# Interleaving the last Strassen products of a hybrid conv/retention layer by token block, and moving its norm steps and weight copies

## What is computed

```python
hcat = x @ w_in                                   # (S, 3584): B, C, h | q, k, v, g
y_conv = b_gate * causal_short_conv(c_gate * hc, conv_w)
o = chunkwise_retention(rotary(q), rotary(k) * 128 ** -0.5, v)     # 4 heads of 128
y_ret = silu(g) * head_group_norm(o, ...)
mix = concatenate([y_conv, y_ret]) @ w_out
x = layer_norm(ALPHA * x + mix, ln1_w, ln1_b)
ff = square(relu(x @ w_ff1)) @ w_ff2              # 1024 -> 4096 -> 1024
ple = sigmoid(x @ w_ple_gate) * (p @ w_ple_proj)  # 256 -> 1024
x = layer_norm(ALPHA * x + ff + ple, ln2_w, ln2_b)
```

## Time and profile before

| what | value |
|---|---|
| device time, median of 3 runs | 792.77 us (791.97 to 793.96) |
| time of the profiled execution | 793.19 us |
| its span, first to last instruction, slowest core | 791.5 us |
| PE busy on that core | 754.2 us (95%) |
| DVE busy | 545.9 us (69%) |
| ACT busy, POOL busy | 304.3 us (38%), 186.7 us (24%) |
| mean rate of the DMA engines | 163 GB/s |

### The profile page before, as it was taken

How to read it: one execution, slowest core, us unless ns; L and a number is a source line. 1 busy time by engine, 2 the same in 40 slices (tenths; PEclk the granted TensorE clock), 3 DMA queues, 4 the chain that set the end, 5 groups by cost and what they waited for, 6 DMA issues and landing times.

```text
span 791.4 us, 12329 instructions; the slowest of 8 cores (787.0 to 791.5 us)
## 1 busy us (share of the span) xinstructions
PE 757.0 (96%) x3896; PEld 357.0 (45%) x3896; DVE 546.3 (69%) x762; ACT 304.3 (38%) x620; POOL 186.3 (24%) x223
## 2 busy tenths in 40 slices
PE   3999999999989999999999999999999999899994
PEld 1444445555545445444444444454444444344441
DVE  4565955648875697798349878835788877765667
ACT  2222226564656307656552100022766752100431
POOL 9100025764455401111110000000443440000011
PEclk9999999999999999999999999999999999999998
DMA  9998048999996251567979668476498676176412
GB/s 130 161 172 186 28 133 107 134 107 113 116 121 202 100 176 55 198 265 251 247 205 157 156 199 200 171 212 188 112 252 274 212 256 224 54 166 146 141 80 107
DMA packets 30352, 128.94 MB, mean 163 GB/s; under 512 B 3728, under 2 KB 5904, under 8 KB 23568
## 3 DMA queue, kind: packets, MB, share of 16 engines
q0 software_dynamic: 9840, 50.34, 39.3%
q1 hardware_dynamic: 19584, 76.23, 28.5%
q10 hardware_dynamic: 864, 1.57, 0.7%
HBM read 131.27 MB, written 45.09 MB: 223 GB/s over the span
## 4 chain that ended last, share of the span: by engine, by line
PE 87%; DVE 5%; DMA 2%; issue 2%; POOL 2%; ACT 1%; DVEq 0%; ACTq 0%; POOLq 0%
PE ps L194 85%; DMA xT_56<-xT 2%; PE ps L198 2%; DVE xacc L212 1%; DVE ycat L201 1%; DVE xacc L201 0%; POOL wc_59 L236 0%; DVE ring_111 L201 0%; POOL wc_60 L236 0%; POOL xT_55 L236 0%; POOL xT_56 L236 0%; ACT sqj L223 0%; POOL lnst L201 0%; DVE tR_143 L201 0%; DVE ra_78 L201 0%
## 5 line engine op out<-in xcount | busy, mean ns | idle before, releaser
L201 DVE TENSOR_TENSOR xacc<-xacc,ps 128x512 f32<-128x512 f32 x80 | 53.0, 685 | 55.7 <-PE ps L194 54.4
L201 POOL TENSOR_TENSOR lnst<-lnst,neghalf 128x1 f32<-128x1 f32 x32 | 26.9, 840 | 138.9 <-DVE lnst L205 87.8
L194 PE MATMUL ps<-ring_106,ycat 128*128 128x512 bf16 x256 | 59.5, 379 | 0.0
L194 PE MATMUL ps<-ring_104,ycat 128*128 128x512 bf16 x224 | 53.1, 388 | 2.6 <-DVE tR_143 L201 2.6
L223 ACT ACTIVATE ycat<-ps 128x1024 bf16<-128x1024 bf16 x16 | 16.3, 1020 | 90.6 <-PE ps L198 90.6
L194 PE MATMUL ps<-ycat,ring_108 128*128 128x512 bf16 x208 | 48.0, 379 | 0.0
L194 PE MATMUL ps<-ycat,ring_109 128*128 128x512 bf16 x208 | 47.8, 379 | 0.0
L201 DVE TENSOR_TENSOR ycat<-hT 128x2048 bf16<-128x2048 bf16 x36 | 43.4, 1222 | 1.5
L201 POOL TENSOR_TENSOR hT<-tR_140 128x512 bf16<-128x512 f32 x15 | 17.5, 1167 | 113.1 <-ACT tR_140 L223 113.1
L194 PE MATMUL ps<-ycat,ring_106 128*128 128x512 bf16 x176 | 41.1, 379 | 0.0
L223 ACT ACTIVATE sg_138<-xacc 128x512 f32<-128x512 f32 x14 | 8.8, 628 | 78.3 <-DVE xacc L201 68.9
(11 more groups left out here) (352 smaller groups left out, 1601.6 us busy)
## 6 DMA issues: line engine op xcount, KB each, us to landing
s_wb<-w_ff POOLq DMA_DIRECT2D x8, 1024.0 KB, 30.4
out<-xacc SPq DMA_DIRECT2D x14, 512.0 KB, 3.4
s_w<-ring_104 SPq DMA_DIRECT2D x10, 512.0 KB, 3.5
s_w<-ring_105 SPq DMA_DIRECT2D x10, 512.0 KB, 3.8
xtmp<-x SPq DMA_DIRECT2D x8, 512.0 KB, 7.3
ring_106<-s_wb POOLq DMA_DIRECT2D x4, 1024.0 KB, 7.7
s_x1f<-xtmp SPq DMA_DIRECT2D x8, 512.0 KB, 4.4
xacc<-s_x1f SPq DMA_DIRECT2D x8, 512.0 KB, 6.2
```

The costliest lines, as they stand in the source:

```text
L194: self.P.op("pe", lambda e: e.matmul(out, lhsT=lhsT, rhs=rhs, start=start, stop=stop, skip_group_check=skip), reads, writes)
L201: self.P.op(eng, lambda e: e.tensor_tensor(out=out, in0=in0, in1=in1, op=op), reads, writes)
```

## The change

- **Copies.** Three of the ten weight copies are issued in the convolution, behind units (2,3), (3,1) and (3,3), the other seven at the end of the retention iterations t = 0, 1, 2, 4, 5, 12 and 13. Each names the tile behind whose write it stands.
- **Norm steps.** In `phase_ff1_last` the stages n = 4, 8 and 12 emit two pieces of the background queue instead of one, and one more piece is emitted behind `last_sums(15)`. All 18 pieces of `gen_outs` then stand ahead of the gate.
- **Last phase.** M1, M3 and M6 stay. M2 and M4 alternate group by group; then come M5_0, M5_1, M7_0, M5_2, M7_1, M7_2, M5_3 (product and token group). The last group, M7_3, runs as two halves of 256 columns in banks 7 and 6, each subtracted and put into the statistics by itself; the statistics of block 3 are four BN_STATS of 256 columns on DVE. `gen_last` waits one piece less before its first operation. M7's slabs are loaded into the ring slots that M2's slabs leave.

The core of the diff:

```diff
-        def copy_bf16(k):
-            h.dma("pool", s_wb[k], w_ff1[k] if k < 8 else w_gate[k - 8], ("wc", k // 4, k % 4), [],
-                  [("s_wb", k)])
+        copies = [0, 4, 1, 5, 2, 6, 3, 7, 8, 9]
+        def copy_bf16(after):
+            k = copies.pop(0)
+            h.dma("pool", s_wb[k], w_ff1[k] if k < 8 else w_gate[k - 8], ("wc", k // 4, k % 4),
+                  [after], [("s_wb", k)])
...
             conv((tt, j))
+            if (tt, j) in ((2, 3), (3, 1), (3, 3)):
+                copy_bf16(("ycat", tt * 4))
...
-            if 1 <= t <= 10:
-                copy_bf16((0, 4, 1, 5, 2, 6, 3, 7, 8, 9)[t - 1])
+            if t in (0, 1, 2, 4, 5, 12, 13):
+                copy_bf16(("kr", t % 2))
...
                 if n >= 2:
-                    bg.step()
+                    bg.step(1 + (n % 4 == 0))
...
             last_sums(15)
+            bg.step()
             product(15, "M6", p, True)
...
-            for m in PRODS[s_]:
+            order = [(m, p, j) for m in ("M1", "M3", "M6") for j, p in JP]
+            groups = [(m, p) for p in range(4) for m in ("M2", "M4")]
+            groups += [("M5", 0), ("M5", 1), ("M7", 0), ("M5", 2), ("M7", 1), ("M7", 2), ("M5", 3)]
+            order += [(m, p, j) for m, p in groups for j in range(2)]
+            slabs = {}
+            for m, p, j in order:
...
+                if (m, j) not in slabs:
+                    slabs[m, j] = use_slab(m, j, min(slab_n["use"] + 5 + (m != "M1"), 30))
+                ff2_product(s_, m, j, p, *slabs[m, j])
+                if j == 1:
+                    ff2_adds(s_, m, p)
+                    if m == "M2":
+                        act_stats(4 + p, 1)
+                        prefetch(30 + 2 * (p == 3))
+                    if m == "M4":
+                        act_stats(4 + p, 0)
+                        bg.add(gen_last(4 + p))
+                    if m == "M5" and p < 3:
+                        act_stats(p, 1)
+                    if m == "M7":
+                        act_stats(p, 0)
+                        bg.add(gen_last(p))
+                bg.step(2 + ((m, p, j) == ("M5", 3, 0)))
+            ff2_add(3, 0, BANK[1]["M5"] + 3, -1)
+            last_stats(3, 2)
+            last_stats(3, 3)
+            for q in range(2):
+                qs = slice(q * 256, (q + 1) * 256)
+                for c in range(16):
+                    lt, rl = left(s_, "M7", c, 3)
+                    slab, rs = slabs["M7", c // 8]
+                    h.mm(ps[7 - q][:, 0:256], lt, slab[:, c % 8, qs], c == 0, c == 15, rl + rs,
+                         [RP[7 - q]])
+                v = xacc[:, 3, qs]
+                h.tt("dve", v, v, ps[7 - q][:, 0:256], ALU.subtract, [RP[7 - q], ("xa", 3)],
+                     [("xa", 3)])
+                last_stats(3, q)
+                if q == 0:
+                    bg.step()
+            bg.add(gen_last(3))
...
             if b != 3:
-                for _ in range(3):
+                for _ in range(2):
                     yield
```

More of the change, by code:

```diff
@@ L1349, in phase_ff2_last @@
                     bg.add(sums[ahead[m]])
-                if m in sums:
+                    del ahead[m]
+                if sums.get(m) in bg.gens:
                     bg.until(sums[m])
[L1352 to L1370, removed]
+                if (m, j) not in slabs:
+                    slabs[m, j] = use_slab(m, j, min(slab_n["use"] + 5 + (m != "M1"), 30))
@@ L1374, in load_x2b, with last_stats @@
                   ("x2b", b % 2), [("s_x1", b)], [("x2b", x2i(b))])
[L1376 to L1380, removed]
+        st24 = lnst[:, 6:8, :].rearrange("p a b -> p (a b)")[:, 0:24]
+        def last_stats(b, k):
+            P.op("dve", lambda e: e.bn_stats(out=st24[:, k * 6:(k + 1) * 6],
+                                             in_=xacc[:, b, k * 256:(k + 1) * 256]),
+                 [("xa", b)], [("lnst", 6), ("lnst", 7)])
         def act_stats(b, hf):
@@ L1402, in gen_last @@
             else:
-                yield from last_stats(b, 0)
-                P.op("dve", lambda e: e.bn_aggr(out=mv, in_=lnst[:, b, 0:12]), [rl], [("mv", b)])
+                P.op("dve", lambda e: e.bn_aggr(out=mv, in_=st24), [("lnst", 6), ("lnst", 7)],
+                     [("mv", b)])
                 h.ts("dve", rstd, mv[:, 1:2], LN_EPS, ALU.add, [("mv", b)], [("rstd", b)])
```

## The result

The changed kernel takes 829.87 us (median of 4 runs, 828.16 to 832.0) against 792.84 us before: a ratio of 1.0468, 95% interval 1.0437 to 1.0498. I had forecast 791.2 us with 787.6 to 796.6; it is 37 us slower. In some executions the cores of one die show a lower granted clock and the time is some per cent longer; every median here leaves these out.

The account below looks back on a forecast made before the run. PE was taken as the bound. Core 0's 791.5 - 1.6 - 2.9 - 1.0 + 1.0 + 0.6 + 2.0 gave 789.6, core 6 789.9; plus 1.7 for the execution, less 0.4 for the median: 791.2 us, range 787.6 to 796.6.

Parts of the forecast that it names:

- The copies: Weight copies issued earlier, in two groups: POOL issues them in idle time, only a load beside them could be late; 0, bounds -1.7 to +1.7.
- The double steps: Two norm pieces at n = 4, 8, 12 delay bank sums: PE waits 1.0 at n = 4, 0.6 for both others.
- the two waits at the end of `phase_ff1_last`: PE's waits for bank sums on DVE go, with no norm piece in stage 15: -1.0 us, bounds 0 and -1.0.
- SP's queue: In `phase_ff1_last`, ring pieces stand behind load1 and out2/load2, which wait for stores to land: +2.0 us, bounds 0 to 7.
- The gate's end: PE's wait ahead of M1 shrinks to 1.20 and the clock stays up: -2.9 us on core 0, -0.5 on core 6.
- The tail: Behind PE's last matmul, the new last-phase order lets DVE end earlier: -1.6 us, bounded by DVE, not PE.
- a thing that would make me wrong: Sign against the forecast: PE waits in the new last phase for banks that DVE has not emptied; no size given.
- The sum: Whole kernel: core 0 ends at 789.6 and core 6 at 789.9, giving a median of 791.2 us.
- The rival of the full stall: On SP, a store's landing holds the pieces fully, at out1 and again at n = 12: 797.6 us, slower; chance 0.20.
- a clock that falls in a new wait: Rival: one core's clock falls again in a new PE wait, costing 1.5 us: 792.7; forecast with fallen clock has chance 0.42.

## Why the prediction was wrong

**The copies.** The step that failed is "The copies", which said that POOL's issue time lies in its idle time and that "a load beside them" was all that could be late: 0, bounds -1.7 and +1.7. I took `[after]` as a mark for the place in POOL's queue. It is a read, and the kernel's bookkeeping lets the next write of that tile wait for its readers, a transfer's until it has landed. The number for that was there, 29.9 us to land, and the loop writes `kr` again after two iterations. I did not set the one beside the other. The read costs 30.3 us with the rest of the change around it (829.9 to 799.6), 28 alone; with the same places and no read it costs nothing. On core 6 the sum is 6.5 + 0.8 + 9.5 = 16.8 of the waits for `kr` (the fourth, 1.1, has its like before), 6.8 at the convolution's end and 8.1 for the clock: 31.7.

**The double steps** were in the sum at 1.6 us and measured 5.7 on core 0 with the copies put back: 1.96, 1.95 and 1.82 behind n = 4, 8 and 12. At n = 4 the 1.0 was the stall without POOL's power; the 0.9 for it stood in the bound and should have been in the sum. 0.57 of what was missing is that wait, and some 0.6 is the second operation, which took 1.92 us and not the 1.28 of the one row I had read; among the eight blocks of core 0 before it took 1.28 to 2.16 (what this hangs on is not shown). At n = 8 and 12 I took 0.6 for both, on the ground of "more slack", from no row; they cost nearly as much as the first. And of the two waits at the end of `phase_ff1_last`, in the sum at -1.0, one of 0.51 is left, so that term came out as -0.5.

**SP's queue.** The mechanism was right and so were both places: load1 waits for out1 (13.1 us) and load2 for out2, and the pieces that M6(8) and M7(8) need stand behind. The size was too small, and it differs by core. With the copies put back there is no such wait on five cores, and there are 3.3, 4.7 and 6.3 us on the other three, where I had 2.0 for all and 0 to 7 as bounds. PE on the slowest, core 4:

```profile
603.15 4.48 PE L194 MATMUL ps<-ycat,ring 128*128 128x512 bf16 x20 [2.98 <-DMA ring<-s_w]
613.51 5.30 PE L194 MATMUL ps<-ycat,ring 128*128 128x512 bf16 x15 [3.28 <-DMA ring<-s_w]
```

On these three cores one bank wait of 1.95 is gone, so that much only changes its name. Behind the second wait 15 matmuls take 5.30 us where they take 3.61 on other cores, at a granted clock of 0.68 in 613.5 to 618.9, so the clock adds 1.7. On core 6 of the changed kernel it was 1.38 + 2.92 and 1.5 for the clock. The time is that of the slowest core, so the upper end was the right one to take: with the load moved away the time falls by 3.9 us. The Trainium skill ("DMA: Bandwidth & Descriptors", section "Anatomy of one DMA — SWDGE (gpsimd) path") says that the wait for a semaphore is done on the issuing sequencer; the SP rows show it, with three transfers standing 13 us behind one that waited, which went out ahead of it where the load was moved. Its price of 3.2 us for the store is an estimate from that section, which is about transfers issued from GpSimd, while out1 goes out on SP. Here out1 took 12.9 us on core 6, with the DMA engines 0.86 busy meanwhile; that this load makes the difference was not tried.

**The gate's end** came out as forecast: 1.3 on all eight cores where I had 1.2, and on all eight the 32 matmuls behind it take 7.07 us, so no clock fell there.

**The tail** came out as forecast behind PE, by the path that was forecast: the span ends 10.05 us behind PE and not 11.7, -1.6, and the last BN_STATS begins 3.7 us ahead of DVE's end, as it was in the sum (3.73). But PE itself ends 1.3 later. M7 adds onto M5's bank, so it must wait until DVE has read it for M5's own addition; in the new order one group lies between the two, and DVE is still at a norm of block 7 (its operation ahead of that add begins at 755.70 on core 4, last phase alone). I had named this as a thing that would make me wrong and not followed the bank table. So the last phase is worth nothing: 1.001 (1.0001 to 1.0019). The wait was named, so the step that failed here is the overlap: the tail was priced as if PE met DVE nowhere earlier in the phase.

**The sum.** 28 to 30 us for the reads, some 6.4 for the norm steps and 0.8 for the last phase make 35 to 37.5, and 37.0 was measured. The rivals of the prediction had the second of these at most; none had the first. The rival of the full stall, at 797.6, is near the 799.59 of the kernel with the copies put back, and a clock that falls in a new wait was seen on core 6 at the 1.5 us that its rival named. Without the copies the forecast would still have been wrong: 799.59 lies above its upper end of 796.6.

## What to carry to other kernels

Where a kernel's bookkeeping orders writes behind reads, a tile named as read by a transfer is held until the transfer has landed, whether the transfer touches it or not: ask of every new dependence who writes that tile next, and set the landing time beside the distance. To hold a place in a queue that works in order, put the transfer behind a small operation on the same engine, or simply behind the instruction that is there already. Background pieces that double an engine's work in one stage are paid by the engine that waits for that stage's results; read the slack of each such stage from its own rows before you price it.

## What was not expected of the hardware

A long idle stretch of PE costs more than itself: behind idle times of 6.5, 6.8 and 9.5 us the granted clock averaged 0.53 to 0.67 in the windows shown, an estimated 2.6 to 2.9 us each, so a quarter to two fifths on top. Behind shorter ones it is not the length alone that decides: with the copies put back the matmuls took 1.7 us longer behind waits of 2.93 us (core 2) and 3.28 us (core 4), and no longer than elsewhere behind 2.98 us (core 4) and 2.74 us (core 3). And the same queue order cost no wait on five cores and up to 6.3 us of waits on another, with the same program: the landing of one store of 512 KB (out1, issue to the issue of load1) took 10.3 us on core 0 and 14.6 us on core 4 with the copies put back.
